# Delta stage: the first projection unit of each following round stands between a group's last state update and its last output turn

## What is computed

```python
p = h @ w_in                        # 1024 -> 6176 columns: q, k, v before the convolution, z, a, b
qkv, buf_new = _causal_conv(p[..., :DN_CONV_CH], buf, conv_w)
qkv = jax.nn.silu(qkv).astype(F32)
z = p[..., DN_CONV_CH:DN_CONV_CH + DN_VW]
def step(s, xs):                    # scan over chunks of 64 tokens, 16 heads of 128x128 state
    qi, ki, vi, gi, bi = xs
    ...
    sol = lax.linalg.triangular_solve(eye + a, rhs, ...)
    u = sol[..., :DN_DV] - sol[..., DN_DV:] @ s
    o = (qi * jnp.exp(G)[..., None]) @ s + att @ u
    s = s * jnp.exp(g_last)[..., None] + jnp.einsum('bhjd,bhjv->bhdv', ki * ..., u)
    return s, o
o = _rms_norm(o, norm_g) * jax.nn.silu(z...)
return o.reshape(B, L, DN_VW) @ w_out, s, buf_new
```

## Time and profile before

| | us |
|---|---|
| median of 3 runs | 2217.83 |
| lowest, highest | 2215.38, 2229.18 |
| profiled execution | 2212.75 |
| its span, first to last instruction | 2210.9 |

### The profile page before, as it was taken

How to read it: one execution, slowest core, us unless ns; L and a number is a source line. 1 busy time by engine, 2 the same in 40 slices (tenths; PEclk the granted TensorE clock), 3 DMA queues, 4 the chain that set the end, 5 groups by cost and what they waited for, 6 DMA issues and landing times. The chain is left out here.

```text
span 2210.9 us, 35700 instructions
## 1 busy us (share of the span) xinstructions
PE 1863.6 (84%) x15037; PEld 971.6 (44%) x15037; DVE 795.4 (36%) x1646; ACT 378.8 (17%) x835; POOL 355.6 (16%) x456
## 2 busy tenths in 40 slices
PE   5999999999899859956989989988987769949970
PEld 3443443433334432324566656755754634433320
DVE  0123323223322330015665465555535323240008
ACT  1010000100000011114332242232232100001111
POOL 0010110101102200022521122032031002120114
PEclk8999999999989979977989989989998779959985
DMA  9364638457170199978321033034035574078964
GB/s 341 123 226 174 255 121 295 164 177 255 68 248 38 43 379 398 398 276 270 129 93 46 15 116 110 12 106 121 8 108 159 177 217 137 27 270 298 403 241 147
DMA packets 234652, 397.20 MB, mean 180 GB/s; under 512 B 17597, under 2 KB 90949, under 8 KB 234438
## 3 DMA queue, kind: packets, MB, share of 16 engines
q1 hardware_dynamic: 228542, 373.43, 48.1%
q0 software_dynamic: 5952, 21.50, 2.6%
HBM read 301.38 MB, written 93.51 MB: 179 GB/s over the span
## 5 line engine op out<-in xcount | busy, mean ns | idle before, releaser
L562 PE MATMUL bank<-ring,hT 128*128 128x512 f32 x768 | 346.5, 602 | 3.3 <-PEq L277 2.2
L562 PEld LDWEIGHTS bank<-ring,hT 128*128 128x128 f32 x768 | 142.8, 191 | 189.2 <-issue 186.5
L1194 PE MATMUL bank<-hT,ring 128*128 128x272 f32 x768 | 220.3, 422 | 0.0
L2344 PE MATMUL bank<-expert_w,exp_xT 128*32 128x512 f32 x1152 | 177.9, 625 | 14.4 <-DMA expert_w<-in_moe_w_gu_dram 10.4
L3020 PE MATMUL bank<-ring,oT 128*128 128x512 f32 x384 | 174.7, 617 | 13.3 <-DMA oT<-oT_spill 12.7
L1194 PEld LDWEIGHTS bank<-hT,ring 128*128 128x128 f32 x768 | 142.8, 199 | 35.0 <-issue 9.5
L1188 PE MATMUL bank<-ring,hT 128*128 128x512 f32 x256 | 125.0, 617 | 0.0
L3020 PEld LDWEIGHTS bank<-ring,oT 128*128 128x128 f32 x384 | 75.4, 198 | 108.0 <-issue 94.9
L2344 PEld LDWEIGHTS bank<-expert_w,exp_xT 128*32 128x32 f32 x1152 | 47.5, 115 | 125.6 <-issue 120.4
L2368 PE MATMUL bank<-expert_w,exp_aT 128*32 128x512 f32 x576 | 88.7, 606 | 10.6 <-DMA expert_w<-in_moe_w_down_dram 9.2
L1864 DVE SCALAR_TENSOR_TENSOR dn_y<-dn_pre,dn_conv,dn_y 128x568 f32<-128x568 f32 x96 | 89.3, 930 | 3.4
(11 more groups left out here) (478 smaller groups left out, 2559.8 us busy)
## 6 DMA issues: line engine op xcount, KB each, us to landing
ring<-in_w_ada_dram SPq DMA_DIRECT2D x24, 2048.0 KB, 9.2
expert_w<-in_moe_w_gu_dram SPq DMA_DIRECT2D x24, 2048.0 KB, 15.8
expert_outputs<-ret_zeros SPq DMA_DIRECT2D x15, 2048.0 KB, 10.4
expert_w<-in_moe_w_down_dram SPq DMA_DIRECT2D x24, 1024.0 KB, 16.3
ring<-in_ret_w_in_dram SPq DMA_DIRECT2D x8, 2048.0 KB, 13.9
ret_Ss<-in_state_ret_dram SPq DMA_DIRECT2D x32, 512.0 KB, 5.5
out_dram<-ret_Ss SPq DMA_DIRECT2D x32, 512.0 KB, 3.9
oT<-in_moe_w_gu_dram SPq DMA_DIRECT2D x8, 2048.0 KB, 21.0
```

Of the source, the lines that this page charges most:

```text
L562: last = pe.matmul(ps[u % 2][:, :], core.hT[:, k, tok(t)], core.ring[:, w % RING, k, :], start=(k == 0), stop=(k == KD - 1))
L1194: mm = pe.matmul(ps[U % 2][:, 0:HALF], core.ring[:, w % RING, k, c * P:(c + 1) * P], core.hT[:, k, half * HALF:(half + 1) * HALF], start=( ...
L2344: last = pe.matmul(ps[v][G * j:G * (j + 1), :], xT[:, v, k, G * j:G * (j + 1)], wgu[of[j] % SLOTS][:, k, :], start=(k == 0), stop=(k == KD ...
```

## The change

In rounds 1 to 3 the last step of the group (C5 of its last chunk) is taken out of the merge. Behind the merged part the eight products of the first unit of the next set are yielded, and then that last C5. The next round leaves these eight products out. The units so moved are U31, U52 (q, k, v units of 128x272 products) and U73 (the sample rows of z, 32 small products). Since `merge` spreads what is left over the same places, all products and steps of rounds 2, 3 and 4 stand a little differently against each other, and those of round 1 too, as its list of steps is one shorter.

```diff
+        first_units = [0] + [10 + 21 * g for g in range(G)] + [len(UNITS)]
+
+        def products(g):
+
+            mm = []
+            for U in range(first_units[g], first_units[g + 1]):
+                for k in range(KD):
+                    mm.append(("mm", U, k))
+                    if k == 3 and U and samples(U - 1):
+                        mm.append(("ST", *unit(U - 1)[0:2]))
+            return mm
+
         def schedule():
 
-            first = [0] + [10 + 21 * g for g in range(G)] + [len(UNITS)]
             for g in range(G + 1):
...
+                mm = products(g)
...
-                elif g < G:
-                    head = 2 * KD if g == 1 else 0
-                    yield from mm[:head]
-                    mm = mm[head:]
-                    yield from merge(group(g - 1), mm, at={1: [SPREAD * (i + 0.5) / len(mm) for i in range(len(mm))]})
+                    continue
+                mm = mm[KD if g > 1 else 0:]
+                head = 2 * KD if g == 1 else 0
+                yield from mm[:head]
+                mm = mm[head:]
+                if g < G:
+                    steps = group(g - 1)
+                    yield from merge(steps[:-1], mm, at={1: [SPREAD * (i + 0.5) / len(mm) for i in range(len(mm))]})
+                    yield from products(g + 1)[:KD]
+                    yield steps[-1]
```

## The result

The change made the kernel slower: a median of 2221.48 us (2216.38 to 2236.86, 12 runs) against 2210.86 us (2197.59 to 2229.18, 12 runs) of before, ratio 1.0048 with a 95% interval of 1.0026 to 1.0071. That is +10.6 us where -8.4 was forecast. The forecast of 2209.4 us stood on the median of the first 3 runs of before, 2217.83; the 12 runs put that kernel 7 us lower. The profiled execution took 2216.38 us (span 2214.6), 3.6 us more than the profiled one of before, so it shows a part of the difference only. In it the four rounds, from the first 128x272 product and then from last C5 to last C5, take 178.6, 181.7, 179.9 and 161.0 us, 701.2 in all, against 181.5, 174.7, 175.4 and 166.0, 697.5 in all, before. Rounds 2 and 3 are longer, by 7.1 and 4.5 us; rounds 1 and 4 are shorter.

A forecast was written before the change was run, and what follows sets the result against it. TensorE, busy 84% of the span, was taken as the bound; -9.45 - 1.8 + 1.3 + 1.5 = -8.4 us took the 2217.83 us median to 2209.4, range 2200 to 2221.

The forecast's parts named there:

- What bounds the kernel: Delta stage: TensorE sets the pace in round 2; the largest wait of rounds 1 to 3, about 6.75 us, precedes the last C5.
- The moved units: Gap before the last C5, rounds 1 to 3: moved products fill it, removing 3.75, 3.75 and 1.95 us later; -9.45 us.
- The clock: Behind the first two gaps, 3.0 us left: the fall to 1.2 GHz remains but is shorter; -1.8 us in all.
- The product that changes sides of C2: Last chunk, rounds 1 to 3: a 128x512 product now precedes C2, so the gap's chain moves 0.43 us later each; +1.3 us.
- The thinner filling: Rounds 2 and 3: 160 instead of 168 products over the same steps, so waits once covered grow; +1.5 us.
- SP: Weight block loads issued behind the dn_S store, some 7 us earlier; nobody waits for the last chunk's store; costed at nothing.
- Slower: the thinner filling drops the clock in new places: Rival: longer C5 and S3 waits in rounds 2 to 4 drop the clock, 3.1 us each; four give 2221.8; chance 0.12.
- Hidden anyway: Rival: steps, not products, set the next round's length, so the moved unit saves nothing; 2217.8 us; chance 0.18.

The follow-up runs named there:

- e1: The changed kernel with only the unit moved, every remaining step and product pinned at its place from before the change: 2203.40 us, 0.43% under before.
- e2: The changed kernel with the last C5 of a round put back ahead of the eight products, the new interleaving kept: 2237.15 us, 1.20% over before.
- e4: The kernel before the change, but POOL waits for the old group's last C5 scaling before making dn_km: 2205.55 us, 0.34% under before.
- e7: The changed kernel with the steps at their old places and the products spread anew: 2209.77 us, 0.17% under before.
- e8: The changed kernel with the remaining products at their old places and the steps at their new ones: 2206.06 us, 0.33% under before.

## Why the prediction was wrong, point by point

**What bounds the kernel.** Right. The gap was there to be filled, and filling it paid wherever nothing else was disturbed (e1) and even where everything was (the changed kernel against e2).

**The moved units, -9.45.** Right. Unit, gap left and chain came out at 3.83, 3.08 (5.07 in round 3) and 7.8 us against 3.75, 3.0 (4.8) and 7.8. e1 has this term and the clock's without the new interleaving: -9.45 - 1.8, and +1.6 for two new bare starts of 0.78 (round 4 began with one before the change too), make -9.7 us; -9.5 was measured, give or take 5.

**The clock, -1.8.** The forecast was that the fall stays and is shorter. In the changed kernel it stayed away behind the first gap. Windows of 8 us behind the three gaps there:

```profile
1274.14:1282.14 8.00, 7.68 (x67) 6.26 (x68) 1.86 (x7) 4.20 (x13) 2.04 (x6) 1.00 1.09 357
1455.86:1463.86 8.00, 7.68 (x60) 6.16 (x61) 0.82 (x2) 2.86 (x8) 0.94 (x3) 0.79 1.09 356
1635.79:1643.79 8.00, 8.00 (x51) 4.70 (x52) 0.42 (x1) 1.83 (x4) 0.94 (x3) 0.63 0.95 343
```

Over the seven kernels with a 3.08 us gap in rounds 1 and 2, such a window showed 1.00 in 3 of 14 cases, 0.79 in 8 and 0.62 in 3; before they were 0.62 and 0.65. That is about 3.2 us at 1.2 GHz on average instead of 5.8, worth 2.6 us for both gaps: the mechanism held more often than not, and -1.8 was somewhat too small. It came near by two errors: 6.44 is the mean of all three low stretches, the third at a gap that the term leaves out (the first two give 5.83), and 4.69 was taken for what is left where 3.2 was measured. And a gap of 1.72 us is no safe one: the earlier trace rows show the C5 of round 2, where the clock stayed at 1.00; behind the same wait in round 1 it was at 0.50 for 8 us, as the section on the result shows. There another wait, of 1.26 us, stands 3.5 us ahead; in rounds 2 and 3 it is 0.81 us.

**The product that changes sides of C2, +1.3.** Mis-sized. The forecast had C3 1.75 us behind C2 (1266.90 to 1268.65); it starts 3.10 us behind (1262.35 to 1265.45), where it was 2.19 before. The third chunk's C5, now 0.87 us nearer to C2, waits 1.55 us in each round where it had not waited, 4.7 us in all. I looked only at `dn_u` and not at this step's own inputs. The product that moved ahead of C2 ends a unit of z, so POOL's multiply of `dn_z` now runs beside the scaling that this C5 waits for, and the scaling takes 2.15 us instead of 1.14: the collision of e4 once more, 1.0 us of the 1.55. VectorE before, then VectorE and POOL of the changed kernel, the same in rounds 2 and 3:

```profile
1265.57 1.14 DVE L1950 SCALAR_TENSOR_TENSOR dn_ob<-dn_ob,dn_rso,dn_z 128x128 f32<-128x128 f32 x4 [1.12 <-POOL dn_rso L1784]
...
1262.75 2.15 DVE L1961 SCALAR_TENSOR_TENSOR dn_ob<-dn_ob,dn_rso,dn_z 128x128 f32<-128x128 f32 x4 [1.12 <-POOL dn_rso L1795]
1263.23 1.26 POOL L1751 TENSOR_TENSOR dn_z<-dn_z,dn_ng 128x512 f32<-128x512 f32 x1 [0.51 <-ACT dn_z L1564]
```

**The thinner filling, +1.5.** This step failed, and carried the sign. It counted products between two steps of TensorE. What mattered is the order of VectorE, where `convolve` hangs on product k = 3 and the steps on their places: a shift of one product against one step puts 3 us of convolution ahead of a waited operation. This also struck the C5 of round 1, which loses no product and for which I took nothing, though that round as a whole came out no longer. In round 3 S3 keeps its six products, as the forecast says, and the second S3 waits 2.96 us more all the same. The new interleaving costs 20 us by e1 against the changed kernel and 27 by e2 against before; without the 4.7 us of the term above, and with the 2.3 us that e1 pays for its three bare starts, that leaves +18 to +22 us for this term instead of +1.5, of which the reversal at the first chunk's C5 is 6 to 9. VectorE's order shows the reversal in three places; the prediction gives it half a sentence.

**SP, 0.** Right: three issues at 1268.12, 4.86 us, and nobody waited for the store.

**The rivals.** "Slower: the thinner filling drops the clock in new places" had the right places (C5 and S3 inside the rounds) and the wrong cause and size: +2.96 us each from a convolution instead of 0.47 or 0.87 from a product, and it stood at 0.12. That its 2221.8 us for four falls is next to the measured 2221.48 is luck: it is +4.0 us on a base of 2217.83, and +10.6 on 2210.86 was measured. "Hidden anyway" gives no gain for the move, and e1 measured 9.5 us. The range ended at 2221, 0.5 us short of the median, and would have missed by more on the base of the 12 runs.

That a convolution stands ahead of the early S3 and solve steps is read from the trace; no run takes it away alone. What stays open is how the rest of the 20 us divides among the early waits of rounds 2 and 3, the third chunk's C5 and the clock; by e7 and e8 it doesn't add up from single shifts, within intervals of some 8 us.

## What to carry to other kernels

When several engines follow one merged list, ask of every shift, also of half a place, what it reverses on each engine's own queue, and compare these orders row by row on the engines that are waited for, not on the bound engine alone. Fill a gap by moving only what fills it and pin all other places; the same move was worth -0.43% with pinned places and +0.48% with places computed from the new lengths. Off-path work in an in-order queue (a convolution nobody waits for soon) lengthens a wait by its full length (2.96 of 2.97 us here) once it lands ahead of an operation that is waited for.

## What the runs showed of the hardware that I had not expected

VectorE's four scalings of 128x128 took 3.13 us beside two POOL multiplies of 128x512 and 1.14 us without them; a wait that put POOL's work 1.3 us later took 0.34% off the kernel before. Beside one POOL multiply of 128x512 they took 2.15 us. Behind a gap of 1.72 us the clock of before was full in rounds 2 and 3 and at 1.2 GHz in round 1. Behind an idle gap of the same 3.08 us TensorE's granted clock was full in 3 of 14 cases and low for a while in 11, so a gap of this length can't be called safe or unsafe for the clock from one profile.
